# Differential attention: VectorE's small operations dealt out between score reads, minima in place of maxima

## What is computed

```python
def blk(qp, q1b, q2b):
    mask = _chunk_mask(qp, kpos)
    dist = jnp.abs(qp[:, None] - kpos[None, :]).astype(f32)
    bias = jnp.where(mask[None], -slopes[:, None, None] * dist[None], NEG)
    s1 = jnp.einsum('bhqd,bhkd->bhqk', q1b, k1).astype(f32) * scale + bias
    s2 = jnp.einsum('bhqd,bhkd->bhqk', q2b, k2).astype(f32) * scale + bias
    a = jax.nn.softmax(s1, axis=-1) - lam * jax.nn.softmax(s2, axis=-1)
    return jnp.einsum('bhqk,bhkv->bhqv', a.astype(v.dtype), v)
```

## Time and profile before

| what | value |
|---|---|
| median of 3 runs | 2602.93 us (2600.15 to 2602.96) |
| the profiled execution: span from first to last instruction | 2600.7 us |
| the profiled execution: own time | not listed apart from the runs above |
| PE busy over the span | 2540.5 us (98%) |
| DVE busy | 1614.7 us (62%) |
| ACT busy | 1212.5 us (47%) |
| stage of differential attention | about 433 to 775 us of the span |
| in it (342 us): PE, DVE, ACT busy | 330.13, 311.65, 250.50 us |

### The profile page before, as it was taken

One profiled execution on the slowest core, in us unless ns is written; L12 is line 12 of the kernel. 1 busy time (PEld: TensorE's weight loads), 2 busy tenths in 40 slices (PEclk: granted clock), 3 DMA queues, 4 the chain that ended last, 5 costly groups with the idle time before them and its releaser, 6 DMA issues.

```text
span 2600.7 us, 35372 instructions
## 1 busy us (share of the span) xinstructions
PE 2540.5 (98%) x12220; PEld 2114.9 (81%) x12220; DVE 1614.7 (62%) x3499; ACT 1212.5 (47%) x2183; POOL 332.0 (13%) x368
## 2 busy tenths in 40 slices
PE   8999999999999999999999999999999999999997
PEld 7998888777667999977877888888888888888886
DVE  6123306998995776654458677876757465564765
ACT  6112314777764555554544333533335353443554
POOL 1110002222221222210000000000000001111143
PEclk9999999999999999999999999999999999999999
DMA  7334458553332111135677767657655365776787
GB/s 232 122 106 125 126 163 253 143 135 87 93 131 90 36 31 45 41 110 158 194 247 220 221 200 237 218 182 216 190 161 179 110 221 108 171 167 162 203 162 137
DMA packets 329436, 398.59 MB, mean 153 GB/s; under 512 B 21408, under 2 KB 235664, under 8 KB 320944
## 3 DMA queue, kind: packets, MB, share of 16 engines
q1 hardware_dynamic: 311696, 364.41, 44.7%
q0 software_dynamic: 17568, 31.99, 8.4%
HBM read 239.86 MB, written 156.48 MB: 152 GB/s over the span
## 4 chain that ended last, share of the span: by engine, by line
PE 62%; DVE 3%; DMA 1%; ACT 1%; issue 1%; SPq 0%; POOL 0%; DVEq 0%; ACTq 0%; POOLq 0%
PE ff_ps_x L3262 26%; PE ff_ps_m L3262 13%; PE ff_ps_z L3262 6%; PE ml_ps_s L2139 6%; PE ff_ps_m L1695 4%; PE ml_ps_o L2168 4%; PE ml_ps_t L2152 2%; DMA ml_v_raw<-scr_yT 1%; DMA ff_pieces<-scr_acc 0%; PE ff_ps_r L2699 0%; PE mo_ps_t L2716 0%; SPq L2326 0%; DVE ff_pieces L2429 0%; DVE ff_pieces L2620 0%; DVE ff_pieces L2616 0%
## 5 line engine op out<-in xcount | busy, mean ns | idle before, releaser
L3262 PE MATMUL ff_ps_x<-ff_mv_hi_p,ff_st_hi_p 128*128 128x512 f32 x764 | 297.8, 390 | 0.5 <-ACT ff_u L3002 0.5
L3262 PE MATMUL ff_ps_x<-ff_mv_hi_p,ff_st_lo_p 128*128 128x512 f32 x764 | 297.3, 389 | 0.0
L3262 PE MATMUL ff_ps_x<-ff_mv_lo_p,ff_st_hi_p 128*128 128x512 f32 x764 | 297.2, 389 | 0.0
L2139 PE MATMUL ml_ps_s<-wide,ml_qs 128*128 128x416 f32 (+14 forms) x880 | 195.6, 356 | 3.7 <-PEq L137 2.7
L3108 DVE TENSOR_TENSOR ff_st_lo_p<-ff_ps_m,ff_st_hi_p 128x512 fp32r<-128x512 f32 x190 | 130.8, 689 | 103.4 <-ACT ff_st_hi_p L2985 103.4
L2952 POOL DMA_DIRECT2D scr_acc<-ff_pieces x64 | 55.5, 872 | 1015.3 <-DVE ff_pieces L3132 946.9
L3002 ACT ACTIVATE ff_u<-ff_ps_x 128x512 f32<-128x512 f32 x128 | 76.6, 598 | 215.0 <-PE ff_ps_x L3262 215.0
L3262 PEld LDWEIGHTS ff_ps_x<-ff_mv_hi_p,ff_st_hi_p 128*128 128x128 f32 x764 | 143.4, 188 | 32.4 <-issue 2.0
L3262 PEld LDWEIGHTS ff_ps_x<-ff_mv_hi_p,ff_st_lo_p 128*128 128x128 f32 x764 | 143.4, 188 | 29.9
L3262 PEld LDWEIGHTS ff_ps_x<-ff_mv_lo_p,ff_st_hi_p 128*128 128x128 f32 x764 | 143.4, 188 | 29.6
L2139 PEld LDWEIGHTS ml_ps_s<-wide,ml_qs 128*128 128x128 f32 x880 | 152.0, 191 | 16.3 <-issue 2.9
(11 more groups left out here) (318 smaller groups left out, 6349.7 us busy)
## 6 DMA issues: line engine op xcount, KB each, us to landing
st_raw<-in_w_ff SPq DMA_DIRECT2D x64, 512.0 KB, 6.2
scr_hid<-ff_pieces SPq DMA_DIRECT2D x128, 256.0 KB, 2.7
st_raw<-scr_hid SPq DMA_DIRECT2D x64, 512.0 KB, 5.4
ring<-in_w_ff SPq DMA_DIRECT2D x28, 1024.0 KB, 7.7
scr_t<-ring SPq DMA_DIRECT2D x24, 1024.0 KB, 5.8
ring<-scr_t SPq DMA_DIRECT2D x21, 1024.0 KB, 8.1
scr_acc<-ff_pieces POOLq DMA_DIRECT2D x64, 256.0 KB, 4.1
ring<-scr_u SPq DMA_DIRECT2D x13, 1024.0 KB, 8.4
```

The lines of the kernel that those rows point to most:

```text
L2139: m = pe.matmul(ps_s[n % NSB][:, 0:w], q, k, start=j == 0, stop=j == len(pairs) - 1)
L3262: m = pe.matmul(bank[:, :], w[kind][:, k], a[kind][:, k], start=start and k == 0 and i == 0, stop=stop and k == KH - 1 and i == 2, skip_gr ...
```

## The change

Four things. (1) The score read multiplies by minus scale and keeps a minimum, so exp is called with scale -1 and no factor is left to apply afterwards; for rows with one chunk (0 to 2) the read writes that minimum straight into `nmax`, and no operation follows. For other rows a TENSOR_REDUCE (`most`) one chunk later takes the minimum of the partial ones. (2) The end of a row is three steps, `invert`, `weigh` and `end`, each at least one chunk apart, at places given by `end_after`; the first inversion comes three chunks after its row, not two. (3) `nmax`, `total`, `inv` have four places, and the second rows 0 to 2 have places of their own in `second`, so that the last row of a head need not be combined before the next head's second rows are read; a wait on `probs_ready` guards the two wide places. (4) `cost` of an end is 100 rather than 250 beyond its width, which shifts PE's transposes and products a little.

```diff
-            return row(i, u) if c == 0 else second[:, i % 2, 0:META + P * (i + 1)]
+            if c == 0:
+                return row(i, u)
+            start, wide = (sum(META + P * (a + 1) for a in range(i)), 0) if i < 3 else (0, i % 2)
+            return second[:, wide, start:start + META + P * (i + 1)]
...
-                        steps += [step for _, step in later if step[2] - NT * step[1] < i]
-                        later = [(left, step) for left, step in later if step[2] - NT * step[1] >= i]
-                        later.append((1, ("exp", 0, i, c)))
+                        due = i if c == COMPS - 1 else i - 1
+                        if i < 3:
+                            due = -1
+                        steps += [step for _, step in later if step[2] - NT * step[1] < due]
+                        later = [(left, step) for left, step in later if step[2] - NT * step[1] >= due]
+                        later += [(1, ("most", 0, i, c))] * (len(row_chunks(i)) > 1) + [(1, ("exp", 0, i, c))]
                         if c == 0:
                             later.append((SCALE_AFTER, ("scale", 0, i)))
                         if c == COMPS - 1:
-                            later.append((END_AFTER, ("end", 0, i)))
+                            later += [(after, (kind, 0, i)) for kind, after in zip(("invert", "weigh", "end"), end_after(i))]
...
+        def end_after(i):
+
+            first = {NT - 1: 5, 0: 3, 1: 3, 2: 3}.get(i) or min(6, 2 * len(row_chunks(i + 1)) - 2)
+            return first, first + 1, first + 2
...
-            return META + P * (step[2] + 1) + 250 if step[0] == "end" else 0
+            return META + P * (step[2] + 1) + 100 if step[0] == "end" else 0
...
-        SCALE_AFTER, END_AFTER = 2, 5
+        SCALE_AFTER = 3
...
-                act.wait_ge(max_ready, NT * COMPS * h + COMPS * i + c + 1)
-                act.activation(comp_row(i, c, u), comp_row(i, c, u), ACT.Exp, bias=nmax[:, i % 2, c:c + 1], scale=scale,
-                               accum_out=total[:, i % 2, c:c + 1]).then_inc(exp_ready, 1)
+                if len(row_chunks(i)) == 1:
+                    act.wait_ge(scores_read, NCH * h + last_chunk(i, c) + 1)
+                else:
+                    act.wait_ge(max_ready, COMPS * (NT - ONE_PART) * h + COMPS * (i - ONE_PART) + c + 1)
+                act.activation(comp_row(i, c, u), comp_row(i, c, u), ACT.Exp, bias=nmax[:, i % 4, c:c + 1], scale=-1.0,
+                               accum_out=total[:, i % 4, c:c + 1]).then_inc(exp_ready, 1)
...
+                if c == 1 and k0 == 0 and not (first_head and i < 4):
+
+                    dve.wait_ge(probs_ready, NT * h + (-1 if i < 3 else 0 if i == 3 else i - 1))
+                least = nmax[:, i % 4, c:c + 1] if w == META + P * (i + 1) else mx[:, i % 4, c, nth:nth + 1]
                 hold(dve, scores_ready, NCH * h + n + 1)
                 dve.tensor_tensor_reduce(out=comp_row(i, c, u)[:, k0:k0 + w], in0=ps_s[n % NSB][:, 0:w],
-                                         in1=bias[u][:, b0:b0 + w], scale=1.0, scalar=LOWEST,
-                                         op0=ALU.add, op1=ALU.max,
-                                         accum_out=mx[:, i % 2, c, nth:nth + 1]).then_inc(scores_read, 1)
-                if k0 + w == META + P * (i + 1):
-                    dve.wait_ge(scores_read, NCH * h + n + 1)
-
-                    dve.tensor_scalar(nmax_all[:, 0:nth + 1], mx[:, i % 2, c, 0:nth + 1], -scale, None, ALU.mult, ALU.min,
-                                      accum_out=nmax[:, i % 2, c:c + 1]).then_inc(max_ready, 1)
+                                         in1=bias[u][:, b0:b0 + w], scale=-scale, scalar=-LOWEST,
+                                         op0=ALU.add, op1=ALU.min,
+                                         accum_out=least).then_inc(scores_read, 1)
...
+            def most(h, i, c, **at):
+                last = last_chunk(i, c)
+                parts = len(row_chunks(i))
+                dve.wait_ge(scores_read, NCH * h + last + 1)
+                dve.tensor_reduce(nmax[:, i % 4, c:c + 1], mx[:, i % 4, c, 0:parts], AX.X, ALU.min).then_inc(max_ready, 1)
```

45 lines of the change are left out of this document (24 added, 21 removed).

## The result

The changed kernel takes **2636.8 us** (median of 4 runs, 2634.0 to 2640.6) against 2601.5 us for the kernel before (4 runs on the same chip): 1.014 times as long, 95% interval 1.0128 to 1.0152. It is 35 us slower, where 3.7 us less were predicted and the range ended at 2606 us.

A forecast was written before the change was run, and what follows sets the result against it. PE was taken as nearly the bound, 81.0 of 86.44 us a head. Gains of 2.4, 1.6, 0.9 and 0.1 us less 1.3 at three borders gave 3.7 us off 2602.93, so 2599 us; range 2592 to 2606.

The forecast's parts named there:

- the change part by part: Part of the prediction pricing small operations, a head's interior, its last scores, the border and the stage's end; 3.7 us less.
- The interior of a head: Inside each head: waits in row 11 and two in head 0 go, 2.4 and 1.6 us; later exponentials stay hidden.
- the wait in row 11: PE's wait in row 11's scores while row 9's combination holds DVE: 0.6 us, four times, forecast to go away.
- The border: Between two heads: combination at E + 5.0, transposes at E + 7.4 us, 0.45 us more lost per border, three borders.
- The stop at the third read: PE's stop before a head's last scores, forecast to move to the new head's third read, about 0.85 us.
- one of the signs that I had set for being wrong: Wrong if the clock row shows 0.5 at a border, the period falls below 84 us or the border's pause under 1.5.
- The head's period: Time of one head in the differential attention stage, 86.44 us before, forecast near 85.5 us.
- The small operations: On DVE: fewer and unchained small operations save 8.4 us a head, DVE's busy time falling to 68 to 76 us.
- the two bounds: DVE's saving a head from the bounds on a small operation's cost: 2.9 to 10.1 us.
- PE as the bound: In the attention stage: PE needs 81.0 of a head's 86.44 us, so relieving DVE gives at most about 21 us.
- Rival C: TensorE's clock halves after pauses of about 2.5 us, 1.7 us a fall; 2604 to 2609 us; chance 0.18.
- Rival D: DVE's chain holds PE inside heads, exponential waits in rows 3 to 5 uncovered, 6.0 us; 2605 and more; chance 0.05.

The follow-up runs named there:

- The run with 16 columns: The changed kernel with POOL scaling only the first 16 columns of every row, same order and waits: 2618.6 us (1.0065).
- the run that restores the time: The changed kernel with POOL's scaling after 4 reads, row 11's finishing steps two reads earlier and row 15's pass one read earlier: 2600.5 us (0.9999).
- the rule of before: The changed kernel, where a row's last read is again followed at once by all steps left of earlier rows: 2634.0 us (1.0133).

## Why the prediction was wrong

**What each edit costs** failed first. In "the change part by part" I priced what VectorE no longer does and gave POOL's moved scaling no term at all; that it costs POOL nothing is right (18.99 and 19.23 us a head), but beside it the pass of VectorE stands still. The order of the changed kernel showed both instructions one read apart, and the trace of before had no row with the two together, so the cost should have been bounded from below by nothing and from above by a whole scaling (POOL's 1.57, 1.67, 1.79 and 1.89 us for rows 11 to 14, four times: 28 us). The run with 16 columns measures it with the order untouched: **18.2 us of the 35**. The run with the scaling one read later gives 24.5, but it moves the first inversion too, and about 5 us of the difference are clock. On VectorE the passes take 108.1 us in place of 87.6. PE pays it in waits: 14.2 us for scores in place of 6.1, the longer wait ahead of rows 8 to 11, and the clock behind these waits.

The Trainium skill has the rule: GPSIMD Engine Reference, Key points, says that POOL shares its SBUF interfaces with VectorE and contends with VectorE instructions that read two SBUF inputs. The traces agree, with the size that the page does not give: all of the overlap but 0.21 us. Score reads, with one input in PSUM, are as long as before also beside POOL (0.58 us for 416 columns, before 0.59).

**The interior of a head** failed second. I said that the wait in row 11 goes away, and gave row 11's own pass, which now stands several reads later, no term. I looked at the row of which the scores are read, not at the place where that pass had moved: PE's transposes of rows 8 to 11 need it, and with the scaling out of the way they still wait 2.17 us. Putting rows 11 and 15 back by two reads and one took 11.8 us more (2612.3 to 2600.5). So the two steps together, 36.3 us, take the changed kernel back to the time of the one before. How they divide depends on the order in which they are taken: row 11 put back first and alone gave 14.1 us.

**The border** was right in its times: 5.0 us, 7.6 us, 2.34 us recorded, as quoted above. The stop at the third read came too, at 1.26 us recorded, more than the 0.85 forecast. Its price was not right: the clock was to stay up, and it fell behind the first and the third border (granted 0.62 from 529 to 533 us and 0.72 from 721 to 725), one of the signs that I had set for being wrong. The head's period, 97.8 and 93.6 us, is not near 85.5 either.

**The small operations** were right in kind and too large in size. (The lower of the two bounds, 2.9 us, should read 3.2.) A reduction that nobody waits for is spaced 0.06 us here, less than the 0.12 taken:

```profile
656.94 0.15 DVE L1564 TENSOR_REDUCE da_nmax<-da_mx 128x1 f32<-128x3 f32 x1
657.00 0.61 DVE L1553 CUSTOM_DVE_ANT_0 da_rows<-da_ps_s,ahead_bias 128x448 f32<-128x448 f32 x1
```

But VectorE's busy time, 79.67 us a head less the 5.1 of the stretched passes, is 74.6, and 73.94 in the run that restores the time. That is inside the predicted 68 to 76, yet 3.8 to 4.5 us below the 78.43 of before and not 8.4; "near 70" was wrong. Part of the rest are short gaps in a chain, which a busy time does not count. For the result it did not matter.

**PE as the bound** was right as far as these runs tell: with 4.5 us a head taken off VectorE and the new waits nearly gone, the time is that of before. The step that failed stands ahead of this one: the kernel as changed had waits that I did not count.

**Rival C** named a true mechanism at too small a size. Within the heads the clock loss grew from nothing to 12.0 us, 8.5 of it in or behind the waits for row 11, pauses of 3.7 us that I had not seen coming, and the run with 16 columns shows that it is not decided by the pause alone. Its chance of 0.18 stopped at 2609. **Rival D** (exponentials too late for VectorE's reciprocals), at 0.05, was the dearest of all wherever the places were moved back: 57 us of waits and 2642 us. The changed kernel avoids it (15.1 us of such waits, before 9.2) by its later places, and these, together with its rule for late steps, are what brings the scaling beside the pass (with the rule of before, at the same places, no pass is stretched). That is the trade in the change: the reduction a read later wants everything behind it later.

## What to carry to other kernels

When a change moves an operation of POOL over SBUF, look in the order of instructions for a two-input pass of VectorE that would start within its duration, and price the whole overlap; if the two must meet and nothing waits for POOL, let VectorE start first. A small operation that releases another engine belongs ahead of the long pass beside it, and its own 0.15 us says nothing of what it costs behind. Taking work off an engine that is not the bound helps only where it shortens a wait of the one that is: here 4.5 us a head off VectorE bought nothing, since PE's waits are for passes at certain places.

## What was not expected of the hardware

- POOL's scaling and VectorE's pass with two inputs in SBUF do not share, they exclude each other: the one that comes second stands still for the overlap less 0.21 us. In these runs POOL 0.18 us ahead, or VectorE 0.02 us ahead, decided which.
- Pauses of PE of nearly the same recorded length (2.10 and 2.17 us at the three borders) were followed by no fall of the clock in one kernel (one profile) and by one each time in the other. What else goes into it stays open.
